# Where one weight tile is rounded in the output projection: three roundings moved behind a layer normalization, one copy moved with them

## The chip, the cores and the metric

The kernel runs on one core of one Trainium2 chip. The metric is the device time of one execution in microseconds (us), the median of several runs. Everything happens in a single launch: four layers of a mixed-attention network and two layers of a retention and stick-breaking network, over 256 rows of 1024 numbers.

## The reference, cut to what matters

The change sits in the middle of each of the first four layers. There the reference computes this (the rest of `first_block` is left out):

```python
for i in range(DEPTH):                      # 4 layers; kinds A, B, C, A
    ...                                     # projections, attention "mix", memory attention "mo"
    mixed = jnp.concatenate([mix.reshape(Bsz, S, MIX_WIDTH), mo.reshape(Bsz, S, MEM_WIDTH)], -1) @ w_out[i]
    x = layer_norm(ALPHA * x + mixed, ln1_g[i], ln1_b[i])
    x = layer_norm(ALPHA * x + swiglu(x, w_gate_up[i], w_down[i]), ln2_g[i], ln2_b[i])

def swiglu(x, w_gate_up, w_down):
    g, u = jnp.split(x @ w_gate_up, 2, axis=-1)
    return (jax.nn.silu(g) * u) @ w_down
```

`w_out` is 1024 x 1024, `w_gate_up` 1024 x 5632, `w_down` 2816 x 1024. All is float32.

## The kernel before

**Products in three passes.** Each float32 operand is split into a rounded part ("high") and the rest ("low"), and a product is three passes on TensorE (PE): high by high, rows' low by weights' high, rows' high by weights' low. The weights come as 264 tiles of 128 x 2048 (1 MB). For each tile SyncE starts a DMA into one of 3 buffers `w_raw` (line 2467), ScalarE (ACT) makes the high part in one of 5 places `w_high` (step `high`, line 1530), and VectorE (DVE) makes the low part `w_low` (step `low`, line 1779). A tile of which a unit of attention comes soon after is made in two halves (`low` and `low_rest`, lines 1779 and 1786; `around` decides it). The DMA of tile t waits for the low of tile t - 3; the high of a tile waits until the tile five places before has been multiplied for both row blocks.

**The order of the work.** A planner (`Plan`) writes one list of steps. Each engine walks through the whole list and issues the instructions of the steps that concern it, in that order, with waits on semaphores; nothing is reordered at run time. `split` is "all owed lows, then one high if a place is free"; `low` is the first half of that, `ahead` is the high alone, `low_one` is one low. While `held` is true, `low` does nothing. `settle` only does bookkeeping.

**The output projection** (`out_and_forward`) multiplies four tiles of `w_out` (tiles 21 to 24 in the first layer, 127 to 130 in the third, 183 to 186 in the fourth): first for rows 0 to 127 (block 0), then for rows 128 to 255 (block 1); in each block the two column halves with the first half of the depth, then both with the second half. The functions `units_on`, `first_rows`, `last_rows` and `rest` run behind the four products of block 0, `rows_turned`, `split`, `turned` and `second` behind those of block 1. What is left of attention runs between them as a background generator: for the last units the scores, exponentials, the transposes of the probabilities (`turn_prob`: PE line 1378, copied out of PSUM by DVE line 2101), the product with the values (`weigh`: PE line 1412, copied out by ACT line 1650) and the splitting of the result into high and low (`mix_split`: ACT line 1657, DVE line 2108). The transposes and the products of the units share two PSUM banks in turn (`tr`): use n can start once use n - 2 has been copied out.

Then comes the residual with the statistics of the norm (DVE lines 1877 and 1884), which also frees one of the two PSUM banks of the large products; the norm itself (`norm`: DVE lines 1860, 1862, 1898, 1910, GpSimd's power at line 2366); the transposes of the normalized rows (PE line 1240) and their splitting (ACT line 1539, DVE line 1813); and the feed-forward stage, whose first tile (25, 131, 187) is the one whose `low` is moved by the change.

**The steps around the change**, as the planner writes them for DVE and ACT. First and fourth layers: product of tile 22, background (copies and exponentials of the last unit's scores), `low 25`, `mix_split` of block 1's first half, product of tile 23, residual, transposes of the last unit, product of tile 24, residual, `weigh` of the last unit, norm of block 0, product of tile 21 for block 1, `mix_split` of block 1's second half, `high 26`, product of tile 22, `low 26`, `high 27`, product of tile 23, `low 27`, splitting of the normalized rows, residual of block 1, product of tile 24, residual, `low 28`, norm of block 1, then the first feed-forward product. Third layer: `low 130`, `high 131`, product of tile 127, background (with the `weigh` copy of unit 19 and the exponentials of unit 21), `low 131`, product of tile 128, background (`weigh` of unit 20, transposes of unit 21), `mix_split`, product of tile 129, residual, `weigh` of unit 21, product of tile 130, residual, norm; from there as in the others.

Of the kernel before, what the change touches and what calls it, by code (L numbers as in the profile page):

```python
# [21 lines left out]
KINDS = "ABCA"  # L22
# [128 lines left out]
class Plan:  # L151
# [624 lines left out]
    def attention(self, layer, gen, keys, values, tail):  # L776


        kind, mix = KINDS[layer], ("mix", layer)
        own = [self.own_units(layer, rb) for rb in range(RB)]  # L780
        mem = [self.memory_unit(layer, rb) for rb in range(RB)]
        ahead = 1 if kind == "A" else 0
        units = self.headed(own[0] + own[1][:ahead] + mem[:1] + own[1][ahead:] + mem[1:], 1)

        def begin():
            self.held = False
            self.on()
            self.drain()
            self.beside(units)
            self.step_background()  # L790

        def keys_turned(rb):
            def then():
                self.background[:] = [self.abreast(self.turn_heads(layer, "k", rb, 2 if kind == "A" and rb == 0 else 1),
                                                   *self.background)]
                self.step_background() if late else self.on()
            return then
        late = kind == "A" and layer
        self.group([keys], gen, [[self.on, keys_turned(0)], [self.step_background if late else self.on, keys_turned(1)]], True)
        if kind == "A":  # L800
            t = [self.tile(*values[:4], 4 * half) for half in range(2)]
            t_tail = [self.tile(tail[0], tail[1], None, "queries", 0)] * 2
        else:
            t_tail, t = [[self.tile(*what[:4], 4 * half) for half in range(2)] for what in (tail, values)]

        def some(n, tiles, where, sort, hooks):
            use = self.gemms.take()
            for half in range(2):
                self.gemm(tiles[half], n, half, gen, "gemm", use, sort, prompt=True)
                if half:  # L810
                    by = ("dve",) * 2 if where[0] in ("qm", "tail") else ("act", "dve")
                    self.evacuate(where, by=by)(n, use, tiles[half])
                hooks[half]()
            return use
        if kind != "A":
            self.blocks[("qm", layer), 0] = some(1, t_tail, ("tail", layer), "tail", [self.on, begin])
        some(0, t, ("proj", layer, 3), "block", [begin if kind == "A" else self.on, self.on])
        if kind == "A":
            some(0, t_tail, ("qm", layer), "queries", [self.on_ahead if layer == LAST else self.on, self.on])
        else:  # L820
            use = some(0, t_tail, ("tail", layer), "tail", [self.on] * 2)
            for rb in range(RB):
                self.blocks[("v", layer), rb] = use

        def first_turned():
            if kind != "B":
                self.step_background()
            self.xt(mix, 0, (0,))
            if kind == "C":
                self.settle()  # L830
            else:
                self.split() if kind == "A" else self.on()

        def turned():
            if kind == "C":
                self.low_one()
                self.ahead()
                self.step_background()
            if kind != "A":
                assert len(self.units[layer, 0]) == len(own[0]) + 1  # L840
                self.xt(mix, 0, (1,))
            self.split() if kind == "C" else self.on()
        some(1, t, ("proj", layer, 3), "block", [first_turned, turned])

    def out_and_forward(self, layer):
        mix = ("mix", layer)
        key = ("ln1", layer)

        def sums(h):
            def then(rb, use, tile):  # L850
                job = Residual(key, rb, h, tile, "gemm", use, True)
                if rb or h == 0 and KINDS[layer] == "B":
                    late.append(job)
                else:
                    self.add("residual", job)
            return then
        late = []

        def units_on():
            self.step_background()  # L860
            if KINDS[layer] == "A":
                self.xt(mix, 0, (1,))
            self.split()

        def first_rows():
            self.step_background()
            if KINDS[layer] == "B":
                self.xt(mix, 1, (0,))
                self.ahead()
            else:  # L870
                self.low_one()
                self.xt(mix, 1, (0,))
                self.settle()

        def last_rows():
            self.step_background()
            if KINDS[layer] == "B":
                self.low_one()
                self.add("residual", late.pop(0))
            else:  # L880
                self.ahead()
            self.split()

        def rest():
            self.drain()
            assert self.units[layer, 1][-1].kind == "mem"
            self.split()
            self.norm(key, 0)
            if layer < LAST:
                self.add("load_kv", layer + 1)  # L890

        def rows_turned():
            self.xt(mix, 1, (1,))
            self.split()

        def turned():
            self.low()
            self.xt(("ff", layer), 0)
            self.add("residual", late[0])
            self.split()  # L900

        def second():
            self.add("residual", late[1])
            self.split()
            self.norm(key, 1)
        self.group([("w_out", layer, h * BLK, "half", sums(h)) for h in range(2)], mix,
                   [[units_on, first_rows, last_rows, rest], [rows_turned, self.split, turned, second]], True)
        self.load_norm(("ln2", layer))
        if layer == LAST:
            self.add("load_second")  # L910
        self.feed_forward(layer)
# [1961 lines left out]
```

## Time and profile before

| what | value |
|---|---|
| median of 3 runs (lowest, highest) | 1551.9 us (1551.57, 1553.08) |
| the profiled execution's own time | 1551.6 us |
| its span in the trace | 1549.8 us |
| mean granted TensorE clock | 0.999 |
| PE busy | 1527.2 us, 99% of the span |
| VectorE busy | 1090.6 us, 70% |
| ScalarE busy | 759.4 us, 49% |
| DMA | 299.87 MB, 193 GB/s |

The span runs from the first to the last instruction of the trace; 1.8 us of the execution's time lie outside it. The busy time of PE is modelled and counts pipelined matmuls, so a short wait inside a run of matmuls can hide in it.

### The profile page before, as it was taken

The page shows a single profiled execution, that of the slowest core. Times are in us where ns is not written, and L with a number is a line of the kernel's source. Part 1 is how long each engine was busy: PE and PEld are TensorE (multiplying, and loading weights), DVE is VectorE, ACT ScalarE, POOL GpSimd, SP SyncE. Part 2 cuts the span into 40 slices and gives each one's busy share as a digit, 9 for nine tenths or more (in the row PEclk, how much of TensorE's full clock was granted, in tenths as well). Part 3 has the DMA queues.
Part 4 walks back from the last instruction along what each step waited for, and adds up shares of the span by engine and source line. Part 5 has one row for each costly group of instructions (what it writes and reads, how often), then busy time and mean ns, then how long its engine had stood idle before and what let it go on. Part 6 is the DMA issues. An engine that isn't in the chain of part 4 may idle for free.

```text
span 1549.8 us, 19849 instructions
## 1 busy us (share of the span) xinstructions
PE 1527.2 (99%) x8091; PEld 1267.2 (82%) x8091; DVE 1090.6 (70%) x1568; ACT 759.4 (49%) x960; POOL 52.8 (3%) x89
## 2 busy tenths in 40 slices
PE   9999999999999999999999999999999999999997
PEld 7887788888878888888788888877888888978986
DVE  6986866656787775677866757888667678567764
ACT  5657444444445443447544433566344434574463
POOL 1100000000000000000000000000100000000010
PEclk9999999999999999999999999999999999999999
DMA  8662566644435766353476654533766646433530
GB/s 323 243 227 83 207 221 263 250 172 181 163 109 193 262 260 250 136 215 112 158 258 226 245 233 143 197 109 137 272 253 240 222 164 224 164 119 140 218 123 27
DMA packets 45898, 299.87 MB, mean 193 GB/s; under 512 B 5540, under 2 KB 5796, under 8 KB 12528
## 3 DMA queue, kind: packets, MB, share of 16 engines
q1 hardware_dynamic: 39600, 278.74, 48.6%
q0 software_dynamic: 5776, 19.01, 3.7%
q8 instruction: 64, 1.05, 0.3%
q10 hardware_dynamic: 432, 0.85, 0.1%
q14 instruction: 26, 0.21, 0.0%
HBM read 296.20 MB, written 2.65 MB: 193 GB/s over the span
## 4 chain that ended last, share of the span: by engine, by line
PE 86%; DVE 8%; ACT 3%; issue 2%; DMA 0%; SPq 0%; POOL 0%; POOLq 0%; DVEq 0%; ACTq 0%
PE psum L1311 55%; PE psum L1270 15%; PE psum L1305 7%; DVE w_low L1779 2%; PE psum L1165 2%; PE psum L1240 1%; PE psum L1424 1%; PE psum L1327 1%; PE psum L1378 1%; PE psum L1308 1%; DVE work L2101 1%; ACT w_high L1530 1%; PE psum L1412 1%; DVE work L2063 1%; DVE w_low L1786 0%
## 5 line engine op out<-in xcount | busy, mean ns | idle before, releaser
L1530 ACT ACTIVATE w_high<-w_raw 128x2048 fp32r<-128x2048 f32 (+1 forms) x240 | 456.3, 1903 | 230.1 <-DMA w_raw<-in_weights 144.6
L1779 DVE TENSOR_TENSOR w_low<-w_raw,w_high 128x2048 fp32r<-128x2048 f32 (+2 forms) x240 | 526.0, 2196 | 40.2 <-ACT w_high L1530 39.2
L1311 PE MATMUL psum<-w_high,xt_high 128*128 128x512 f32 (+1 forms) x1376 | 378.6, 395 | 1.3 <-ACT xt_high L1539 1.3
L1311 PE MATMUL psum<-w_high,xt_low 128*128 128x512 f32 (+1 forms) x1376 | 368.4, 388 | 0.3 <-DVE xt_low L1813 0.3
L1311 PE MATMUL psum<-w_low,xt_high 128*128 128x512 f32 (+1 forms) x1376 | 368.1, 388 | 0.0
L1311 PEld LDWEIGHTS psum<-w_high,xt_low 128*128 128x128 f32 x1376 | 257.4, 188 | 54.8 <-DVE xt_low L1813 0.7
L1311 PEld LDWEIGHTS psum<-w_low,xt_high 128*128 128x128 f32 x1376 | 257.3, 188 | 54.0 <-DVE w_low L1765 0.5
L1311 PEld LDWEIGHTS psum<-w_high,xt_high 128*128 128x128 f32 x1376 | 249.8, 188 | 52.1 <-ACT xt_high L1539 1.8
L2130 DVE TENSOR_TENSOR arena<-arena,psum 128x256 f32<-128x256 f32 x88 | 37.0, 420 | 203.5 <-ACT arena L1665 203.1
L1665 ACT ACTIVATE arena<-psum 128x256 f32<-128x256 f32 x88 | 33.7, 383 | 217.7 <-PE psum L1311 217.7
L1270 PE MATMUL psum<-w_high,ht_high 128*128 128x512 f32 x352 | 99.9, 401 | 0.0
L1270 PE MATMUL psum<-w_high,ht_low 128*128 128x512 f32 x352 | 96.1, 390 | 0.0
L1270 PE MATMUL psum<-w_low,ht_high 128*128 128x512 f32 x352 | 95.9, 390 | 0.0
L1270 PEld LDWEIGHTS psum<-w_high,ht_low 128*128 128x128 f32 x352 | 66.1, 188 | 14.4
L1270 PEld LDWEIGHTS psum<-w_low,ht_high 128*128 128x128 f32 x352 | 66.1, 188 | 14.1
L1270 PEld LDWEIGHTS psum<-w_high,ht_high 128*128 128x128 f32 x352 | 63.2, 188 | 11.0
L1562 ACT ACTIVATE arena<-psum 128x512 f32<-128x512 f32 (+1 forms) x51 | 28.7, 568 | 83.9 <-PE psum L1311 46.4
L1802 DVE SCALAR_TENSOR_TENSOR arena<-w_raw,c_col,arena 128x512 f32<-128x512 f32 x84 | 62.9, 749 | 2.6
L2366 POOL TENSOR_TENSOR norm_rstd<-norm_rstd,half_neg 128x1 f32<-128x1 f32 (+1 forms) x32 | 23.5, 735 | 1124.6 <-DVE norm_rstd L1862 869.3
L1922 DVE TENSOR_SCALAR arena<-psum 128x512 f32<-128x512 f32 x28 | 19.3, 689 | 47.8 <-PE psum L1311 24.4
L1606 ACT ACTIVATE work<-work,neg_max 128x128 f32<-128x128 f32 (+3 forms) x80 | 38.1, 477 | 24.2 <-DVE neg_max L2063 23.7
L1813 DVE TENSOR_TENSOR xt_low<-psum,xt_high 128x512 fp32r<-128x512 f32 (+1 forms) x48 | 31.0, 673 | 17.0 <-ACT xt_high L1539 16.3
(253 smaller groups left out, 1498.5 us busy)
## 6 DMA issues: line engine op xcount, KB each, us to landing
w_raw<-in_weights SPq DMA_DIRECT2D x260, 1024.0 KB, 4.8
norm_params<-in_ln_g POOLq DMA_DIRECT2D x8, 512.0 KB, 4.2
norm_params<-in_ln_b POOLq DMA_DIRECT2D x8, 512.0 KB, 5.9
w_raw<-in_weights SPq DMA_DIRECT2D x4, 656.0 KB, 6.4
kv_outside<-arena POOLq DMA_DIRECT2D x3, 512.0 KB, 5.8
mem_kv<-kv_outside POOLq DMA_DIRECT2D x3, 512.0 KB, 3.5
norm_params<-mods_outside POOLq DMA_DIRECT2D x3, 512.0 KB, 5.9
x_rows<-in_x SPq DMA_DIRECT2D x4, 256.0 KB, 5.6
```

What stands on the lines that cost most here:

```text
L1165: m = e.matmul(pieces[n][1], left, right, start=banks[i] not in banks[:i], stop=banks[i] not in banks[i + 1:])
L1270: m = e.matmul(psum[:, K.wide.place(j.use) + h, :], left[:, c, rb * P:rb * P + P], right[:, w:w + BLK], start=first and c == 0 and n == 0, ...
L1305: m = e.matmul(dst, right[:, c + b * P:c + b * P + P], rows[:, kk, :], start=first and b == 0, stop=last and b == 1)
L1311: m = e.matmul(psum[:, bank, 0:w], rows[:, kk, rb * P:rb * P + P], right[:, at:at + w], start=first, stop=last)
L1530: e.activation(K.w_hi[:, g % RING, 0:w], K.w_raw[:, r, 0:w], ACT.Copy).then_inc(K.high.hit(t), 1)
L1562: m = e.activation(to, out, ACT.Silu if j.silu else ACT.Copy, scale=K.evac_scale(j.where, j.rb))
L1606: m = e.activation(pr, pr, ACT.Exp, bias=K.negmax[:, slot, n:n + 1], scale=-1.0, accum_out=K.expsum[:, slot, n:n + 1])
L1665: e.activation(K.ff_silu[j.step % 2][:, j.rb, :], psum[:, K.gemms.place(j.use), 0:FF_STEP], ACT.Silu).then_inc(K.silu_done.hit((j.layer, j ...
L1779: m = e.tensor_tensor(K.w_lo[:, s, 0:n], K.w_raw[:, r, 0:n], K.w_hi[:, s, 0:n].bitcast(F32), ALU.subtract)
L1802: m = e.scalar_tensor_tensor(out=acc, in0=w, scalar=c, in1=acc, op0=ALU.mult, op1=ALU.add)
L1813: m = e.tensor_tensor(lo[at], psum[:, K.tr.place(j.use), 0:n * P].rearrange("p (c s) -> p c s", s=P), hi[at].bitcast(F32), ALU.subtract)
L2130: e.tensor_tensor(K.ff_h[j.step % 2][:, j.rb, :], K.ff_silu[j.step % 2][:, j.rb, :], bank[:, FF_STEP:BLK], ALU.mult).then_inc(K.gemms.sem( ...
```

## The change

Three edits in the planner. They change no instruction and no operand, only the places of three `low` steps and of one `high` step in the list:

```diff
@@ attention, the hook behind the last product of the values @@
-            self.split() if kind == "C" else self.on()
+            self.low() if kind == "C" else self.on()
@@ out_and_forward, units_on @@
-            self.split()
+            if KINDS[layer] == "C":
+                self.ahead()
+            else:
+                self.split()
@@ out_and_forward, first_rows, kinds A and C @@
-                self.low_one()
+                self.held = True
                 self.xt(mix, 1, (0,))
                 self.settle()
@@ out_and_forward, rest @@
             self.split()
             self.norm(key, 0)
+            self.held = False
+            self.low()
```

In the first and fourth layers (kind A) the low of the first feed-forward tile (25, 187) goes from in front of `mix_split` of block 1's first half to behind the norm of block 0, and thus in front of `mix_split` of block 1's second half. In the third layer (kind C) the low of tile 131 goes the same way, and the high of tile 131 goes from in front of the product of tile 127 to in front of the product of tile 128, behind the background work between them. In the second layer (kind B) no low is owed at that place, and the list stays as it is.

## Rows read from the trace of the kernel before

**Rows 1.** The page, part 4: chain that ended last, by engine.
```profile
PE 86%; DVE 8%; ACT 3%; issue 2%; DMA 0%; SPq 0%; POOL 0%; POOLq 0%; DVEq 0%; ACTq 0%
```

**Rows 2.** Waits of PE over the span: us in total, times, longest.
```profile
PE psum L1412 <- DVE work L2101: 2.0, 2, 1.0
...
PE psum L1240 <- DVE arena L2119: 1.7, 1, 1.7
...
PE psum L1378 <- ACT arena L1650: 1.0, 1, 1.0
```

**Rows 3.** PE timeline, first layer: start, us, instruction, [idle before <-releaser].
```profile
163.43 1.08 PE L1311 MATMUL psum<-w_low,xt_high 128*128 128x512 f32 x4
165.49 1.09 PE L1412 MATMUL psum<-work,mem_kv 128*64 128x128 f32 x16 [0.98 <-DVE work L2101]
...
178.44 1.19 PE L1311 MATMUL psum<-w_high,xt_high 128*128 128x512 f32 x4
```

**Rows 4.** Timeline of DVE, first layer.
```profile
159.94 2.28 DVE L1779 TENSOR_TENSOR w_low<-w_raw,w_high 128x2048 fp32r<-128x2048 f32 x1
162.15 0.68 DVE L2108 TENSOR_TENSOR xt_low<-arena,xt_high 128x512 fp32r<-128x512 f32 x1
...
164.07 1.27 DVE L2101 TENSOR_SCALAR work<-psum 128x512 f32<-128x512 f32 x2
165.26 0.68 DVE L1877 SCALAR_TENSOR_TENSOR x_rows<-x_rows,psum 128x512 f32<-128x512 f32 x1
...
169.87 0.68 DVE L2108 TENSOR_TENSOR xt_low<-arena,xt_high 128x512 fp32r<-128x512 f32 x1
171.57 2.29 DVE L1779 TENSOR_TENSOR w_low<-w_raw,w_high 128x2048 fp32r<-128x2048 f32 x1 [1.02 <-ACT w_high L1530]
174.30 2.29 DVE L1779 TENSOR_TENSOR w_low<-w_raw,w_high 128x2048 fp32r<-128x2048 f32 x1 [0.43 <-ACT w_high L1530]
...
177.71 0.68 DVE L1877 SCALAR_TENSOR_TENSOR x_rows<-x_rows,psum 128x512 f32<-128x512 f32 x1
```

**Rows 5.** Timeline of PE's weight loads, first layer.
```profile
178.43 0.76 PEld L1311 LDWEIGHTS psum<-w_high,xt_high 128*128 128x128 f32 x4 [0.28 <-DVE x_rows L1877]
```

**Rows 6.** Timeline of ACT, third layer.
```profile
742.23 1.90 ACT L1530 ACTIVATE w_high<-w_raw 128x2048 fp32r<-128x2048 f32 x1
744.03 0.36 ACT L1650 ACTIVATE arena<-psum 128x256 f32<-128x256 f32 x1
...
747.76 0.91 ACT L1625 ACTIVATE work<-work,recip 128x256 f32<-128x256 f32 x2 [0.48 <-DVE recip L2077]
748.92 0.38 ACT L1650 ACTIVATE arena<-psum 128x256 f32<-128x256 f32 x1 [0.25 <-PE psum L1412]
```

**Rows 7.** Timeline of PE, third layer.
```profile
744.44 0.66 PE L1378 MATMUL psum<-ident,work 128*128 128x128 f32 x4 [1.00 <-ACT arena L1650]
...
748.82 1.20 PE L1378 MATMUL psum<-ident,work 128*128 128x128 f32 x8
...
755.67 1.07 PE L1311 MATMUL psum<-w_low,xt_high 128*128 128x512 f32 x4
...
762.92 1.07 PE L1311 MATMUL psum<-w_high,xt_low 128*128 128x512 f32 x4
```

**Rows 8.** Timeline of DVE, third layer.
```profile
746.36 1.28 DVE L2101 TENSOR_SCALAR work<-psum 128x512 f32<-128x512 f32 x2
...
748.38 2.28 DVE L1779 TENSOR_TENSOR w_low<-w_raw,w_high 128x2048 fp32r<-128x2048 f32 x1
...
756.78 0.69 DVE L1877 SCALAR_TENSOR_TENSOR x_rows<-x_rows,psum 128x512 f32<-128x512 f32 x1 [2.55 <-PE psum L1311]
...
761.40 0.69 DVE L2108 TENSOR_TENSOR xt_low<-arena,xt_high 128x512 fp32r<-128x512 f32 x1
...
767.63 0.68 DVE L1877 SCALAR_TENSOR_TENSOR x_rows<-x_rows,psum 128x512 f32<-128x512 f32 x1
```

**Rows 9.** Weight DMAs (line 2467), whole span: issue to landing.
```profile
DMA to landing us min/median/max: 3.8/4.8/9.4
```

## The prediction

> **What bounds the kernel.** The chain of waits read back from the end runs over PE for 86% of the span [rows 1], so a step on another engine costs or gives time only where PE waits for it. The list of PE's waits is short [rows 2]. Two of them touch this change. PE's product of the last unit's probabilities with the values waits twice, 2.0 us together, for DVE's copy at line 2101: once in the first layer (0.98 us) [rows 3] and once at the same place of the fourth. PE's transposes wait once 1.00 us for ACT's copy at line 1650; that is the third layer [rows 7]. Then the timelines say who causes them. First layer: DVE does the moved `low` at 159.94, and everything behind it comes 2.21 us later, the copies among them (164.07) [rows 4]. Third layer: ACT does `high 131` from 742.23, and the copy that PE wants starts only at 744.03 [rows 6].
>
> The decisive view is a fourth one, PE's weight loads. The first feed-forward product's load starts at 178.43, after 0.28 us of waiting for the residual at line 1877 [rows 5], which frees the PSUM bank. That residual starts at 177.71 and lasts 0.68 [rows 4]. So at the end of the stage PE is already just caught by DVE (the same wait stands once in each of the four layers), and what PE gains earlier counts only if this residual comes earlier too. For each layer I therefore reckon two clocks, PE's and DVE's, up to this point.
>
> **First and fourth layers (the low behind the norm).** Nothing is added or removed; one low of 2.21 us (162.15 - 159.94) changes place on DVE. In front of it the unit's copies are no longer held up: they come after ACT's split at 160.8, the `mix_split` low (0.60), residual and statistics (1.3), so at about 162.7 instead of 164.07, and end by 164.0. PE ends the product of tile 24 one group after 163.43, at 164.5, and goes on with no wait, at 164.43 instead of 165.49 [rows 3]: PE gains 1.06 us here. DVE gains less: the second residual now waits for PE's product. In the third layer such a residual comes 1.11 us after the start of the last group of the product before it (755.67 to 756.78) [rows 7, 8]; here that gives 163.43 + 1.11 = 164.54 instead of 165.26. From this residual to the one that PE waits for, DVE before took 177.71 - 165.26 = 12.45 us, of which it waited 1.10 (171.57 - 169.87 - 0.60) and 0.52 (174.30 - 171.57 - 2.21) for ACT's highs [rows 4]; 10.83 is work. After the change the low stands in this stretch, 13.04 of work, and it fills the two waits: the highs are ready by then, since PE frees their places 1 us earlier. 164.54 + 13.04 = 177.58, against 177.71. So the bank comes free 0.13 us earlier, and of PE's 1.06 us only 0.13 is kept. The 0.9 us left becomes a longer wait of the first feed-forward product for line 1877. The bounds: at best the whole 1.06 (if that product didn't need the bank), at worst about 0. I take -0.13 for each of the two layers, -0.26 together.
>
> **Third layer, the high.** `high 131` (1.80 us from start to next start, 742.23 to 744.03) goes behind the background work. Gain: ACT copies unit 19 at once, PE's transposes no longer wait, and the product of tile 128 starts 1.1 us earlier. But PE's next step, the product of unit 20, needs DVE's copies at 746.36, which hang on DVE's own chain, and in the first layer such a product follows the start of the two copies by 1.42 us (164.07 to 165.49) [rows 3, 4]. That gives 747.78; the transposes behind it start at 748.82 before [rows 7], and so they do after. The gain is spent in a wait there: 0. Loss: on ACT the high now stands behind the scaling at 747.76 (0.82 to the next instruction) and in front of the copy of unit 20's product, which was at 748.92 [rows 6]. High from 748.58 to 750.38, copy at 750.38, 1.46 us later. That copy frees the bank of the second group of unit 21's transposes. Where PE waited for such a copy before, it began 0.41 us after the copy's start (744.03 to 744.44) [rows 6, 7]; now 750.79, against 748.82 + 0.41 = 749.23 without a wait. PE's product of tile 129 starts another 0.41 us on: 751.20, against 748.82 + 0.95 (eight transposes without a wait) = 749.77. PE loses 1.43 us. Bounds: 0, if something else already held PE there (no row says so), and 1.8, the whole high. I take 1.43.
>
> **Third layer, the low.** Before, `low 131` ran at 748.38, while DVE had room: it later waited 2.55 us for PE [rows 8]. This low delayed nothing that PE wanted. After, it stands behind the norm, where DVE is the tight one. The second residual follows PE: 756.78 + 1.43 = 758.21. The norm ends 4.62 us on (761.40 - 756.78): 762.83. The low to 765.04; the `mix_split` low from 765.04 to 765.73. PE wants this for the second pass of tile 129, which started at 762.92 [rows 7], so now 764.35: it waits some 1.5 us there. Then the two lows, the splitting and the residual follow without a gap as before (767.63 - 761.40 = 6.23 [rows 8]): 765.04 + 6.23 = 771.27, against 767.63. The bank comes free 3.64 us later: 1.43 from the high and 2.21 from the low. PE, delayed by some 3 us by then, waits for the rest. Bounds of the low's part: 0 (if PE had slack of 2.2 us at the residual, but it was waiting already) and 2.3. I take 2.21, thus +3.64 for the layer.
>
> **What hides nothing and what could.** The DMAs of tiles 28, 134 and 190 wait for the moved lows. In the first layer tile 28 is asked for at 171.4 instead of 162.2, lands 4.8 us later (median) [rows 9], at 176.2, and its high ends near 178.2; its low is due near 180.2. Third layer: 765.1 + 4.8 + 1.9 = 771.8, due near 773.9. Some 2 us of room: cost 0, up to 2.6 if a landing took the longest 9.4 us [rows 9]. Behind the stage PE is the bound again, and nothing there gives a delay back.
>
> **Sum.** -0.26 + 3.64 = +3.38 us, against the profiled execution's 1551.6 (span 1549.8 and 1.8 outside): 1555.0. The median shown is 0.3 higher, so 1551.9 + 3.4 = 1555.3. In this kernel 0.2% is 3.1 us, about what a measurement can tell from no change; the bound lies at 1555.0, just under the forecast.
>
> **The rivals.**
> 1. Faster: the three PE waits go and stay gone, 1.06 + 1.06 + 1.1 = 3.2 us, 1548.7. It decides at the bank wait: it needs the residual at line 1877 not to hold PE. Against it speaks the 0.28 us wait of the weight load [rows 5], which shows that PE already arrives before the bank is free. Chance 0.07.
> 2. Half of the third layer's loss: the high is harmless (ACT or the banks leave more room than I see) and only the low costs, 2.21 - 0.26 = +2.0, 1553.9; or the other half alone, +1.2. For it: a stall of 1.4 us is put together from steps of different units. Chance 0.18.
> 3. No effect, the lists come out alike in time, 1551.9. Against it: in the third layer the low leaves a stretch with a gap of 2.55 us and enters one without. Chance 0.05.
> 4. Late weights: a landing as long as the longest delays a low by some 2.5 us in one layer; 1551.9 + 3.4 + 2.5 = 1557.8. Chance 0.09.
> 5. The granted clock falls at the new waits. PE's longest wait of this kind is 1.7 us [rows 2] with a mean granted clock of 0.999, and mine are no longer than 1.5, which speaks against it. If the third layer's stretch of some 20 us ran at 1.2 GHz, half the speed, it would cost some 10 us more: 1565. Chance 0.03. The Trainium skill ("TensorE: Matmul & The Clock Gate", section "A second HAM failure mode: psum-queue depth-cycling") says that frequent short idles between groups of matmuls, where PSUM banks are cycled, can make the clock swing between its two levels; that is the shape of these waits, and the trace of before doesn't show it happening.
>
> **How the numbers follow.** The forecast has 0.58, with an own range of 1554.5 to 1556.0; about seven tenths of it lie over 1555.0. Slower by over 0.2%: 0.41 of it, with rivals 4 and 5 0.53. Faster: 0.07. The rest, 0.40, is within. The range from 1553.3 to 1557.6 takes in the forecast, most of rival 2 and a part of rival 4.
>
> **What would show it.** First layer: no PE wait for line 2101; the wait of the weight load for line 1877 grown from 0.28 to about 1 us (0.6 to 0.9 of PE's); that residual at 177.6. Third layer: the PE wait of 1.00 for ACT's line 1650 gone from 744.44, a new one of about 1.3 before the second transposes of unit 21 near 750.8; DVE's residual near 771.3 and the first feed-forward product 3.6 us later; a new wait of PE for line 2108. All three layers together are wrong if the feed-forward product of the third layer comes less than 3 us later, and the forecast of slower is wrong if line 1877 no longer stands among what PE's weight loads wait for.

## The result, and the profile after

The changed kernel takes 1555.04 us (median of 14 runs, 1554.07 to 1556.77), the kernel before on the same chip 1552.12 us (14 runs). The ratio is 1.0018, with a 95% interval from 1.001 to 1.0025: slower by 2.9 us. The profiled execution took 1554.92 us with a span of 1553.1 us, 3.3 us longer than the span before. Forecast were 1555.3 us and +3.4. (A ratio is worked out with its interval from the single runs; it need not be the quotient of the two medians.)

Each engine has exactly the instructions it had, and the granted clock is the same 0.999. In what follows the lines of the changed kernel are numbered 5 higher than before (1882 is the residual of line 1877, 2106 the copies of 2101, 1655 the copy of 1650, 2113 the split of 2108); in the rows shown of the experiments' kernels the same lines stand 4 to 10 higher than before, by what their own edits add. The waits of PE over the span, us in total, times, longest, with those that answer to [rows 2]:

```profile
PE psum L1245 <- DVE arena L2124: 1.7, 1, 1.7
...
PE psum L1316 <- DVE x_rows L1882: 1.3, 3, 0.5
...
PE psum L1383 <- ACT arena L1655: 1.3, 1, 1.3
PE psum L1316 <- DVE xt_low L2113: 1.3, 1, 1.3
...
PE psum L1417 <- DVE work L2106: 1.0, 1, 1.0
```

The wait for the copies is down from 2.0 to 1.0, and even this 1.0 isn't what is left of the old ones: it is a new one in the third layer. The wait for ACT's copy grew from 1.0 to 1.3, and two new names stand in the list: the residual, and the low of the mixed rows. The list's sum does not show the loss: it is 14.2 us before and 14.3 after, because two waits at the program's start (1.3 us for ACT at 6.96, 0.3 for DVE at 7.80) are missing from this execution, and because part of what a wait costs stands only with the weight loads. The stages have to be read one by one.

**First layer.** PE's timeline, answering to [rows 3]:

```profile
164.40 1.09 PE L1417 MATMUL psum<-work,mem_kv 128*64 128x128 f32 x16
...
172.06 1.21 PE L1316 MATMUL psum<-w_high,xt_low 128*128 128x512 f32 x4
...
178.26 1.20 PE L1316 MATMUL psum<-w_high,xt_high 128*128 128x512 f32 x4 [0.44 <-DVE x_rows L1882]
```

DVE's timeline, answering to [rows 4]:

```profile
164.51 0.69 DVE L1882 SCALAR_TENSOR_TENSOR x_rows<-x_rows,psum 128x512 f32<-128x512 f32 x1 [0.53 <-PE psum L1316]
...
169.12 2.29 DVE L1784 TENSOR_TENSOR w_low<-w_raw,w_high 128x2048 fp32r<-128x2048 f32 x1
171.32 0.69 DVE L2113 TENSOR_TENSOR xt_low<-arena,xt_high 128x512 fp32r<-128x512 f32 x1
...
177.53 0.68 DVE L1882 SCALAR_TENSOR_TENSOR x_rows<-x_rows,psum 128x512 f32<-128x512 f32 x1
```

and two of PE's weight loads, of which the second answers to [rows 5]:

```profile
172.06 0.77 PEld L1316 LDWEIGHTS psum<-w_high,xt_low 128*128 128x128 f32 x4 [0.43 <-DVE xt_low L2113]
...
178.26 0.76 PEld L1316 LDWEIGHTS psum<-w_high,xt_high 128*128 128x128 f32 x4 [0.86 <-DVE x_rows L1882]
```

At 164.40 PE goes on without a wait, 1.09 us earlier than before. The moved low starts at 169.12 on DVE, in front of the split of the mixed rows, and at 172.06 PE's weight load waits 0.43 us for that split, which takes back 0.25 of the 1.09 us. At 178.26 PE is only 0.18 us ahead: its weight load has waited 0.86 us for the residual where it waited 0.28, because the residual came at 177.53 instead of 177.71.

**Third layer.** ACT's timeline, answering to [rows 6]:

```profile
742.65 0.38 ACT L1655 ACTIVATE arena<-psum 128x256 f32<-128x256 f32 x1 [0.58 <-PE psum L1417]
...
747.52 0.91 ACT L1630 ACTIVATE work<-work,recip 128x256 f32<-128x256 f32 x2 [0.48 <-DVE recip L2082]
748.33 1.90 ACT L1535 ACTIVATE w_high<-w_raw 128x2048 fp32r<-128x2048 f32 x1
750.13 0.36 ACT L1655 ACTIVATE arena<-psum 128x256 f32<-128x256 f32 x1
...
769.82 1.92 ACT L1535 ACTIVATE w_high<-w_raw 128x2048 fp32r<-128x2048 f32 x1 [0.60 <-DMA w_raw<-in_weights]
```

PE's, answering to [rows 7]:

```profile
747.54 1.09 PE L1417 MATMUL psum<-work,arena 128*64 128x128 f32 x16 [1.03 <-DVE work L2106]
748.57 0.66 PE L1383 MATMUL psum<-ident,work 128*128 128x128 f32 x4
750.55 0.66 PE L1383 MATMUL psum<-ident,work 128*128 128x128 f32 x4 [1.32 <-ACT arena L1655]
...
765.53 1.21 PE L1316 MATMUL psum<-w_high,xt_low 128*128 128x512 f32 x4 [1.25 <-DVE xt_low L2113]
...
771.73 1.20 PE L1316 MATMUL psum<-w_high,xt_high 128*128 128x512 f32 x4 [0.44 <-DVE x_rows L1882]
```

and DVE's, answering to [rows 8]:

```profile
757.97 0.69 DVE L1882 SCALAR_TENSOR_TENSOR x_rows<-x_rows,psum 128x512 f32<-128x512 f32 x1 [2.55 <-PE psum L1316]
...
762.59 2.28 DVE L1784 TENSOR_TENSOR w_low<-w_raw,w_high 128x2048 fp32r<-128x2048 f32 x1
764.79 0.69 DVE L2113 TENSOR_TENSOR xt_low<-arena,xt_high 128x512 fp32r<-128x512 f32 x1
...
770.99 0.68 DVE L1882 SCALAR_TENSOR_TENSOR x_rows<-x_rows,psum 128x512 f32<-128x512 f32 x1
```

Read these in order of time. ACT copies unit 19's product at once (742.65), and PE saves its 1.0 us; it spends it at 747.54 in a wait for DVE's copies. The high then sits at 748.33 in front of ACT's next copy (750.13), and PE waits 1.32 us for that. The low sits at 762.59 in front of the split of the mixed rows, PE waits 1.25 us for it, and 0.44 more at 771.73 for the residual that came behind it all. The high of tile 134 waited 0.60 us for its DMA at 769.82, but its low had room.

**The table of the stage.** PE's list is the same in all kernels of this document, so one can take the start of the same two matmuls in each trace, one before the moved steps and one behind the whole stage (the transposes of block 1's normalized rows), and compare the time between them. This leaves out whatever differed elsewhere in that execution. Before: 28.41 us in the first layer (158.34 to 186.75), 26.80 in the second, 33.88 in the third (742.78 to 776.66), 28.43 in the fourth. Where a kernel's list is that of before, the difference is at most 0.06 us, which shows how steady these times are. The differences in us, and beside their sum the ratio of the timed runs with its interval:

| kernel | first | second | third | fourth | sum | ratio of times (95%) |
|---|---|---|---|---|---|---|
| changed | -0.19 | 0.01 | 3.61 | -0.19 | 3.24 | 1.0018 (1.001 to 1.0025) |
| e1_a_only | -0.18 | 0.00 | 0.03 | -0.17 | -0.32 | 0.9997 (0.9988 to 1.0005) |
| e2_c_only | -0.01 | 0.01 | 3.62 | 0.06 | 3.68 | 1.0025 (1.0016 to 1.0034) |
| e3_c_low | 0.01 | 0.01 | 2.20 | 0.01 | 2.23 | 1.001 (1.0001 to 1.0018) |
| e4_c_high | -0.01 | 0.03 | 1.43 | 0.03 | 1.48 | 1.0007 (0.9998 to 1.0016) |
| e5_before_bank | -0.17 | -0.12 | -0.12 | -0.18 | -0.59 | 0.9998 (0.999 to 1.0007) |
| e6_after_bank | -0.92 | -0.13 | 2.89 | -0.92 | 0.92 | 1.0006 (0.9997 to 1.0016) |
| e7_a_later_bank | -1.23 | -0.12 | -0.11 | -1.23 | -2.69 | 0.9979 (0.9969 to 0.9989) |
| e8_c_copies | -1.23 | -0.12 | -1.23 | -1.25 | -3.83 | 0.9975 (0.9966 to 0.9984) |

The first four experiments were timed on one chip and the last four on another, each four beside the kernel before on the same chip; the changed kernel was timed apart from both. Three slow runs (5694 us of `e6_after_bank`, 2283 and 6727 us of the kernel before beside it) are left out of the ratios, but not of the medians given for the last four.

### The profile page after: what moved, and what is told of

It reads as the page before. It is cut to its first block, busy times and chain, and to the rows that moved or that the text cites. A ratio compares the mean times of both kernels' runs of the same rounds, so it can differ in the third digit from the quotient of the medians.

```text
span 1553.1 us, 19849 instructions
## 1 busy us (share of the span) xinstructions
PE 1529.9 (99%) x8091; PEld 1267.8 (82%) x8091; DVE 1090.8 (70%) x1568; ACT 759.2 (49%) x960; POOL 52.2 (3%) x89
## 3 DMA queue, kind: packets, MB, share of 16 engines
q8 instruction: 64, 1.05, 0.3%
## 4 chain that ended last, share of the span: by engine, by line
PE 84%; DVE 9%; ACT 3%; issue 2%; DMA 1%; SPq 0%; POOL 0%; POOLq 0%; DVEq 0%; ACTq 0%
PE psum L1316 52%; PE psum L1275 15%; PE psum L1310 7%; DVE w_low L1784 3%; PE psum L1170 2%; PE psum L1429 1%; PE psum L1245 1%; PE psum L1383 1%; PE psum L1332 1%; PE psum L1417 1%; DMA w_raw<-in_weights 1%; PE psum L1313 1%; ACT w_high L1535 1%; DVE xt_low L1818 1%; DVE x_rows L1882 1%
## 5 line engine op out<-in xcount | busy, mean ns | idle before, releaser
L1544 ACT ACTIVATE xt_high<-psum 128x512 fp32r<-128x512 f32 (+1 forms) x48 | 26.7, 587 | 34.6 <-PE psum L1245 34.1
```

Of the source, the lines that this page charges most:

```text
L1544: m = e.activation(hi[:, 4 * j.g:4 * j.g + n, j.rb * P:j.rb * P + P], psum[:, K.tr.place(j.use), 0:n * P].rearrange("p (c s) -> p c s", s= ...
```

## The experiments

The theory: in the first and fourth layers, the time is set by when DVE's residual frees the PSUM bank, and in the third by the place of the high in ACT's queue and of the low in DVE's. The rivals: removed PE waits are gained; late weights (the DMA three tiles on waits for the moved low) are what costs.

**The two parts of the change alone.** `e1_a_only` has only the first and fourth layers' part, `e2_c_only` only the third's:

```diff
 # e1_a_only, against the change: the hooks of kind C as before
-            self.low() if kind == "C" else self.on()
+            self.split() if kind == "C" else self.on()
...
-            if KINDS[layer] == "C":
-                self.ahead()
-            else:
-                self.split()
+            self.split()
 # e2_c_only, against the change: kind A as before
-                self.held = True
+                if KINDS[layer] == "C":
+                    self.held = True
+                else:
+                    self.low_one()
```

Behind its `self.held = True` the `e1_a_only` kernel lets the third layer's low go where it was: none is owed there by then.

> Only the first and fourth layers' part of the change: low 25 and low 187 behind the norm, the third layer as before. Bank-and-queue theory (what counts is when DVE's residual at the end of the projection frees the PSUM bank): PE's wait of 0.98 us for the copies goes in both layers, but each keeps only about 0.15 us; about 0.3 us faster than the kernel before, no change that can be measured. Theory that removed PE waits are gained: 2.1 us faster (ratio 0.9986). Theory of late weights (the DMA three tiles on waits for the moved low): slower by about 1 us per layer.

> Only the third layer's part: high 131 one step later, low 131 behind the norm. Bank-and-queue theory: +3.6 us against before (ratio 1.0023), which with the first and fourth layers' -0.3 gives the whole change. If the slowdown were spread over all layers or were something outside this stage: +1.1 us or less.

Measured: 1551.42 us (ratio 0.9997) and 1555.85 us (1.0025) against 1552.58. The first median looks like a gain of 1.2 us, but the ratio's interval (0.9988 to 1.0005) holds no change; the last section says where the medians get such a shift from. In the stages, -0.18 and -0.17 in the first and fourth layers for the one, +3.62 in the third for the other. The whole slowdown is the third layer's, and the parts add up to the changed kernel's (3.24 against -0.32 + 3.68 = 3.36). "Removed waits are gained" wanted -2.1 us from the first: it falls, since the trace of it has no wait for the copies in these layers and yet keeps only 0.2 us of each. Late weights wanted a loss of about 1 us in each of these layers, and there is none.

**The third layer's two moves alone.**

```diff
 # e3_c_low, against e2_c_only: the high keeps its place, only the low is moved
-            self.low() if kind == "C" else self.on()
+            self.split() if kind == "C" else self.on()
...
-                self.ahead()
+                self.settle()
 # e4_c_high, against the change: the high moved, the low behind unit 21's copies
-                self.held = True
+                self.low_one()
```

> Third layer: high 131 stays in its old place, only low 131 goes behind the norm. Bank-and-queue theory: +2.2 us (one low of DVE's time added where DVE has no gap), with PE's wait for ACT's copy (1.00 us) still there; ratio 1.0014. Late weights: the DMA of tile 134 waits for this low as in the whole change, so the whole +3.6 us would be here.

> Third layer: high 131 one step later as in the change, low 131 right behind unit 21's copies instead of behind the norm. Bank-and-queue theory: +1.4 us, from PE's wait for ACT's copy of unit 20's product growing out of the one that goes; ratio 1.0009; it and the low alone add up to the third layer's whole. Late weights: the low is only 4 us later than before, with 7 us of room, so 0. Theory that removed waits are gained: -1.0 us.

Measured: 1553.92 (1.001) and 1553.7 us (1.0007); in the stage +2.20 and +1.43 us, together 3.63 against 3.62 for both at once. DVE's timeline of `e3_c_low`, whose PE had no shift up to the norm: the low is in front of the split of the mixed rows, and no gap stands from there to the residual.

```profile
760.88 2.28 DVE L1787 TENSOR_TENSOR w_low<-w_raw,w_high 128x2048 fp32r<-128x2048 f32 x1
763.09 0.69 DVE L2116 TENSOR_TENSOR xt_low<-arena,xt_high 128x512 fp32r<-128x512 f32 x1
763.69 4.49 DVE L1787 TENSOR_TENSOR w_low<-w_raw,w_high 128x2048 fp32r<-128x2048 f32 x2
768.09 1.28 DVE L1821 TENSOR_TENSOR xt_low<-psum,xt_high 128x512 fp32r<-128x512 f32 x2
769.29 0.68 DVE L1885 SCALAR_TENSOR_TENSOR x_rows<-x_rows,psum 128x512 f32<-128x512 f32 x1
```

PE's waits of `e4_c_high` in the third layer's stage are the two that the high makes, without those of the low:

```profile
PE psum L1383 <- ACT arena L1655: 1.3, 1, 1.3
PE psum L1417 <- DVE work L2106: 1.0, 1, 1.0
```

So the high costs 1.43 and the low 2.20. Late weights wanted all of it with the low and nothing with the high: both are wrong. "Removed waits are gained" wanted -1.0 from `e4_c_high`: wrong in sign.

**The bank at the end of the projection.** The four further kernels share one other order at the end: the residual that frees the bank comes first, the second low behind it, and the norm of block 1 in front of the next low.

```diff
 def turned():
-            self.low()
-            self.xt(("ff", layer), 0)
             self.add("residual", late[0])
+            self.xt(("ff", layer), 0)
             self.split()
 def second():
             self.add("residual", late[1])
-            self.split()
             self.norm(key, 1)
+            self.split()
```

`e5_before_bank` is the kernel before with it, `e6_after_bank` the changed one.

> The kernel before, with one other order at the end of the projection in all four layers: DVE does block 1's first residual, which frees the PSUM bank, before the splitting of the normalized rows and before the second low (27, 80, 133, 189), and the norm of block 1 before the next low. Bank theory: the weight load's wait of 0.28 us at the first feed-forward product goes in four layers, 0.15 us each: 0.6 us faster (ratio 0.9996), near nothing, since before the change PE arrives only just too early. Late weights or DVE-bound norm: slower by up to 1 us per layer.

> The changed kernel with that same order at the end. The moved lows stay behind the norm, so late weights stay late. Bank theory: the first and fourth layers now keep about 0.9 us each of the 1.06, the third loses 2.8 instead of 3.6 (1.4 for the copy, 1.5 for the mixed rows' low, less 0.15), the second gains 0.15: together +0.9 us against before (ratio 1.0006), 2.4 us faster than the changed kernel. Late weights as the cause of the slowdown: +3 us against before, as the change has it.

Measured: 1552.38 (0.9998) and 1553.66 us (1.0006) against 1552.38. This is the pair that shows the bank. (The pair also moves the norm of block 1. But the gain is there already when PE starts the first feed-forward product, at 179.38 in the rows below, and in that trace DVE starts the norm of block 1 only at 182.12.) The order alone gives 0.12 to 0.18 us per layer; on top of the change it raises what the first and fourth layers keep from 0.19 to 0.92, and brings the third from 3.61 to 2.89. Neither timed ratio can be told from no change; it is the traces that tell the two kernels apart. PE's first feed-forward product in the first layer of `e6_after_bank` is the second of these rows, and it waits for nothing (this execution came to the stage 1.7 us later than that of before, so its times are higher):

```profile
178.48 1.07 PE L1315 MATMUL psum<-w_low,xt_high 128*128 128x512 f32 x4
179.38 1.07 PE L1315 MATMUL psum<-w_high,xt_high 128*128 128x512 f32 x4
```

and in its third layer the wait for the residual is gone, the other three are not:

```profile
PE psum L1382 <- ACT arena L1654: 1.3, 1, 1.3
PE psum L1315 <- DVE xt_low L2112: 1.3, 1, 1.3
PE psum L1416 <- DVE work L2105: 1.1, 1, 1.1
```

The moved lows are as late as in the change, and late weights expected +3 us from this kernel; its stages give +0.92.

**A version that is faster.** `e7_a_later_bank` adds to that order, on the kernel before, only what helped: the low of the first feed-forward tile in the first and fourth layers goes behind the norm and also behind the split of the mixed rows that PE wanted at 172.06 of the changed kernel. `e8_c_copies` takes the third layer in hand too.

```diff
 # e7_a_later_bank, against the kernel before, beside the order above
-                self.low_one()
+                if KINDS[layer] == "A":
+                    self.held = True
+                else:
+                    self.low_one()
...
             self.xt(mix, 1, (1,))
+            self.held = False
             self.split()
 # e8_c_copies, against e7, where the list is finished
+        move(("low", 130), lambda what, job: what == "turn_prob" and job[0].n == 20)
+        move(("low_rest", 130), lambda what, job: what == "recip" and job.n == 21)
+        move(("high", 131), lambda what, job: what == "mix_split" and job[:3] == (("mix", 2), 1, 0))
+        move(("low", 131), lambda what, job: what == "residual" and job[:3] == (("ln1", 2), 0, 0))
```

(`move` puts a step right behind the last step for which the condition holds.)

> That order at the end in all layers; low 25 and low 187 behind the norm and also behind the splitting of the mixed rows' second half; the third layer's low and high as before. Bank theory: 1.2 us from each of the first and fourth layers (1.06 and the 0.15), 0.15 from each of the others: 2.7 us faster than before (ratio 0.9983). If the bank is not what bound: 0.3 us.

> As the kernel that goes before it in this list, and in the third layer DVE does unit 21's maxima and unit 20's copies before low 130, whose halves come behind the copies and behind unit 21's reciprocals; high 131 comes behind the splitting of the mixed rows, low 131 behind the first residual, where ACT and DVE had gaps of 4.0 and 2.5 us. If unit 20's product waits for DVE's chain there (the reason given why the 1.00 us of PE's wait was not gained): another 1.1 us, 3.8 us faster than before (ratio 0.9975). If the wait for ACT's copy was the only one: no more than the kernel ahead of it.

Measured: 1548.87 us, ratio 0.9979 (0.9969 to 0.9989), and 1548.04 us, ratio 0.9975 (0.9966 to 0.9984). The stages give -2.69 and -3.83 us, and both kernels are faster than the one before, by intervals clear of 1, while the changed one is slower by such an interval. That `e8_c_copies` is also faster than `e7_a_later_bank` is told by the stages alone (third layer -1.23 against -0.11); their timed ratios overlap. In the third layer of `e8_c_copies` DVE does unit 20's copies in front of the low of tile 130, and the transposes of units 20 and 21 on PE both run without a gap (eight in 1.21 us each); the low of tile 131 sits where DVE had waited for PE, with 0.36 us of that wait left:

```profile
742.66 1.28 DVE L2111 TENSOR_SCALAR work<-psum 128x512 f32<-128x512 f32 x2
743.85 1.22 DVE L1789 TENSOR_TENSOR w_low<-w_raw,w_high 128x1024 fp32r<-128x1024 f32 x1
...
751.61 2.28 DVE L1789 TENSOR_TENSOR w_low<-w_raw,w_high 128x2048 fp32r<-128x2048 f32 x1
754.24 0.69 DVE L1887 SCALAR_TENSOR_TENSOR x_rows<-x_rows,psum 128x512 f32<-128x512 f32 x1 [0.36 <-PE psum L1321]
```

The 1.00 us of PE's wait for ACT's copy [rows 7] was there to be had, but only with both waits taken away: the change took away one and the second stood right behind it.

## Why the prediction was right, step by step

- **First and fourth layers.** Forecast: 1.06 us gained by PE in front, 0.13 kept. Measured: 1.09, and 0.19 kept. The reason was the bank; `e6_after_bank` shows it, where the same move keeps 0.92. The prediction expected the other 0.9 us as a longer wait for line 1877, 0.6 to 0.9 of it as PE's own. PE's own wait is 0.44, and the weight load's grew by 0.58: 0.25 of the gain had already gone at 172.06, in the wait for the mixed rows' low, which the prediction passed over in these layers. It changed nothing in the sum while the bank bound; without the bank's wait it is the small rest of 0.3 us between `e6_after_bank` (0.92) and `e7_a_later_bank` (1.23), where the low stands behind that split and PE goes on without this wait.
- **Third layer, the high.** Forecast +1.43, measured +1.43 (`e4_c_high`). That the two agree to the hundredth is partly luck, since the sum is put together from steps of other units and layers; but both halves held: the gain goes into the wait for DVE's copies, forecast at 747.78 and found at 747.54 (this execution was 0.24 us ahead when it came to the stage), and the copy of unit 20 is late by the high's length less what ACT had spare.
- **Third layer, the low.** Forecast +2.21, measured +2.20 (`e3_c_low`). The low left a stretch where DVE waited 2.55 us for PE and went into one without a gap. PE's wait for the mixed rows' low was forecast as some 1.5 us, though its own figures give 765.73 - 764.35 = 1.38; the trace has 1.25. The size of this wait doesn't enter the sum, because the residual behind it decides.
- **DMAs.** Forecast 0: the landing comes later, but inside the room. Tile 134's high waited 0.60 us for its DMA where it had waited for none, tile 135's 1.99 us where it had waited 0.92, and nothing waited for these highs: DVE has no gap in front of their lows.
- **Sum.** Forecast +3.38, the stages +3.24, the spans +3.3, the medians +2.9. The difference of the last is within the interval.
- **The rivals.** The faster one fell with `e1_a_only`, half a loss with `e3_c_low` and `e4_c_high` (either alone is real, but they add up), late weights with `e6_after_bank`. The clock stayed at 1.00 through the third layer's stage with waits of up to 1.3 us, so the rival of the clock didn't come at this place. It exists at another one (last section).

The chances need a word too. The prediction put the bound of 0.2% at 3.1 us and gave 0.53 to a slowdown above it and 0.40 to a change within it. The measured ratio of 1.0018 lies just within, with an interval (1.001 to 1.0025) that holds the bound. So the size, inside the forecast's own range of 1554.5 to 1556.0, came out, and on which side of the bound it fell is not decided by these runs.

## What to carry to other kernels

A wait of the bounding engine is worth its length only if nothing else holds the engine before the next place where it must meet the others. Follow both clocks, the bounding engine's and that of the one it waits for, from the edit to the next meeting point, here the residual that frees a PSUM bank, and look there whether a weight load already waits a little. Here 0.28 us of such a wait said that the bank was already what held PE, and the sum along DVE's own chain said how much of 1.06 us would arrive: 0.13 forecast, 0.19 measured. When work is moved along an in-order queue, look for the queue's own gaps: the low of tile 131, moved from in front of a gap of 2.55 us into a stretch with none, cost its full 2.2 us, and moved into that gap in `e8_c_copies` it cost nothing that the stage shows.

## What the runs showed that was not expected

In four of the ten profiled executions (`e1_a_only`, `e3_c_low`, `e5_before_bank`, `e8_c_copies`) PE's clock fell for some 3 us at one and the same place, the first product of the retention layers near 1286 us, where the kernels do the same work. Busy time of the engines and the granted clock (the column behind POOL) in stretches of `e1_a_only`:

```profile
1280.00:1285.80 5.80, 4.00 (x21) 2.68 (x19) 5.07 (x7) 1.76 (x5) 0.55 (x1) 1.00 0.54 181
1285.80:1289.10 3.30, 3.30 (x11) 2.57 (x10) 2.56 (x6) 0.60 (x1) 2.18 (x4) 0.54 0.56 184
1289.10:1295.00 5.90, 5.90 (x29) 4.86 (x28) 4.60 (x6) 3.39 (x3) 0.00 (x0) 0.97 0.73 297
```

and of the kernel before:

```profile
1280.00:1286.10 6.10, 4.30 (x21) 2.91 (x20) 5.37 (x7) 2.18 (x5) 0.55 (x1) 1.00 0.46 164
1286.10:1288.90 2.80, 2.80 (x15) 2.35 (x14) 2.10 (x4) 0.60 (x1) 2.19 (x4) 1.00 0.47 147
```

At 0.54, about the lower of the clock's two levels (1.2 GHz of 2.4), four matmuls took 1.6 and 1.7 us from start to start where they take 0.9 to 1.0. In front of it PE was busy 4.00 of 5.80 us, with two waits of 1.07 and 0.73 us; in the kernel before, busy 4.30 of 6.10 with the same waits, the clock stayed. All ten traces have these two waits, 1.05 to 1.08 and 0.73 us long, and only four have the fall, so the waits alone do not decide it; what does is not shown. The Trainium skill ("TensorE: Matmul & The Clock Gate", section "A second HAM failure mode: psum-queue depth-cycling") says that frequent short idles between groups of matmuls can make the clock swing between its two levels. The four traces agree in so far as the fall comes right behind two such idles.

Each fall cost 1.5 to 1.6 us, half of what this change is worth. The timed runs look as if it came and went in them too, which no trace of theirs can show: those of `e1_a_only` lie in two groups, seven from 1551.0 to 1551.7 us and four from 1552.7 to 1553.2, and its profiled run, the one with the fall, is in the upper group. The runs of the kernel before on that chip have the same gap, 16 up to 1552.4 us and 16 from 1552.8, and their median of 1552.58 lies in it; a median can thus move by 1.2 us where the stages show a gain of 0.3. The fall is not the only such source: `e6_after_bank` has no fall, but came to its first output projection 1.7 us late, from a stretch at 113 to 118 us in which PE waits for DVE (0.45 and 0.84 us). This is why the stages were compared between two fixed matmuls and not by the spans: `e1_a_only` has a span 1.6 us longer than the kernel before, and a stage sum 0.3 us shorter.
